# Two transformer blocks on one core: own buffers for each stage's first two weight units, their loads before the attention's end, and a later turn of the second row tile

## What is computed

```python
# block 0, per layer
proj = rmsnorm(x, g_pre_mix) @ w_in                      # 1024 x 3404
mix  = concat(top-k, forgetting, differential, window attention)
x = x + rmsnorm(mix @ w_out, g_post_mix)
x = x + rmsnorm(square(relu(rmsnorm(x, g_pre_mlp) @ w_up)) @ w_down, g_post_mlp)
x = x + sigmoid(x @ w_ple_gate) * (p_i @ w_ple_proj)
# block 1, per layer
z = x @ w_in_2 + b_in_2                                  # 1024 x 11648
mix = (sigmoid(ga) * (attn @ w_ap) + sigmoid(gb) * (silu(g) * retention @ w_rp)) @ w_out_2
x = layer_norm(ALPHA * x + mix)
x = layer_norm(ALPHA * x + (silu(x @ w_gate) * (x @ w_up)) @ w_down)
```

## Time and profile before

| | us |
|---|---|
| median of 3 runs | 2001.11 |
| profiled execution | 1996.49 |
| its span | 1994.7 |
| TensorE busy | 1905.3 (96%) |
| VectorE busy | 1172.4 (59%) |
| ScalarE busy | 887.9 (45%) |

### The profile page before, as it was taken

One profiled execution on the slowest core, in us unless ns is written; L12 is line 12 of the kernel. 1 busy time (PEld: TensorE's weight loads), 2 busy tenths in 40 slices (PEclk: granted clock), 3 DMA queues, 4 the chain that ended last, 5 costly groups with the idle time before them and its releaser, 6 DMA issues.

```text
span 1994.7 us, 25098 instructions
## 1 busy us (share of the span) xinstructions
PE 1905.3 (96%) x9135; PEld 1564.7 (78%) x9135; DVE 1172.4 (59%) x1372; ACT 887.9 (45%) x1071; POOL 82.3 (4%) x97
## 2 busy tenths in 40 slices
PE   7988999999899999999999989998999999989997
PEld 6777888778678887888877778886888877778885
DVE  5775555667765456556566565445556566574445
ACT  5544444555344445444345334443344355434442
POOL 5300000022100000000000000000000000000000
PEclk9989999999799999999999999999999999999998
DMA  7404555553755555664455644555663455645553
GB/s 260 141 15 154 189 183 166 177 190 113 86 190 195 182 174 181 216 213 124 143 189 173 224 152 160 186 184 190 213 215 122 147 185 191 209 149 164 186 186 106
DMA packets 194402, 340.25 MB, mean 171 GB/s; under 512 B 9338, under 2 KB 59418, under 8 KB 194316
## 3 DMA queue, kind: packets, MB, share of 16 engines
q1 hardware_dynamic: 189072, 327.76, 50.0%
q0 software_dynamic: 5120, 11.15, 3.1%
q10 hardware_dynamic: 123, 0.14, 0.0%
HBM read 333.24 MB, written 5.77 MB: 170 GB/s over the span
## 4 chain that ended last, share of the span: by engine, by line
PE 83%; DVE 8%; ACT 3%; DVEq 3%; issue 2%; DMA 1%; SPq 0%; ACTq 0%
PE G L580 18%; PE G L581 18%; PE G L585 18%; PE T L634 5%; PE A L580 4%; PE A L581 4%; PE A L585 4%; PE G L602 2%; PE G L596 2%; PE G L597 2%; DVE wlo L1544 2%; ACT whi L1090 2%; PE T L684 1%; PE A L694 1%; ACT arena L1090 1%
## 5 line engine op out<-in xcount | busy, mean ns | idle before, releaser
L1544 DVE TENSOR_TENSOR wlo<-raw,whi 128x2048 fp32r<-128x2048 f32 (+2 forms) x316 | 666.7, 2111 | 617.9 <-ACT whi L1090 617.4
L1090 ACT ACTIVATE whi<-raw 128x2048 fp32r<-128x2048 f32 (+3 forms) x320 | 566.0, 1769 | 647.1 <-PE G L585 523.8
L580 PE MATMUL G<-whi,XH 128*128 128x512 f32 (+1 forms) x1408 | 560.8, 398 | 8.3 <-DVE XL L1568 6.6
L581 PE MATMUL G<-whi,XL 128*128 128x512 f32 (+1 forms) x1408 | 550.3, 391 | 0.0
L585 PE MATMUL G<-wlo,XH 128*128 128x512 f32 (+1 forms) x1408 | 346.2, 388 | 0.0
L580 PEld LDWEIGHTS G<-whi,XH 128*128 128x128 f32 x1408 | 266.7, 189 | 64.8 <-issue 8.4
L581 PEld LDWEIGHTS G<-whi,XL 128*128 128x128 f32 x1408 | 266.7, 189 | 54.1 <-issue 1.9
L585 PEld LDWEIGHTS G<-wlo,XH 128*128 128x128 f32 x1408 | 263.9, 188 | 53.6
L634 PE MATMUL T<-ident,arena 128*128 128x128 f32 x812 | 120.7, 289 | 25.5 <-ACT arena L1090 18.1
L634 PEld LDWEIGHTS T<-ident,arena 128*128 128x128 f32 x812 | 99.3, 148 | 45.3 <-ACT arena L1090 15.3
L1090 ACT ACTIVATE arena<-T 128x512 f32<-128x512 f32 (+2 forms) x92 | 46.2, 550 | 151.2 <-PE T L634 150.9
(11 more groups left out here) (225 smaller groups left out, 2066.7 us busy)
## 6 DMA issues: line engine op xcount, KB each, us to landing
raw<-in_w_in SPq DMA_DIRECT2D x112, 1024.0 KB, 6.7
raw<-in_w_mlp_up SPq DMA_DIRECT2D x32, 1024.0 KB, 5.4
raw<-in_w_mlp_down SPq DMA_DIRECT2D x32, 1024.0 KB, 5.0
raw<-in_w_ffn_gate SPq DMA_DIRECT2D x44, 512.0 KB, 4.0
raw<-in_w_ffn_up SPq DMA_DIRECT2D x44, 512.0 KB, 5.0
raw<-in_w_ffn_down SPq DMA_DIRECT2D x44, 512.0 KB, 3.3
raw<-in_w_out SPq DMA_DIRECT2D x16, 1024.0 KB, 5.0
raw<-in_w_ret_proj SPq DMA_DIRECT2D x16, 1024.0 KB, 5.1
```

The lines of the kernel that those rows point to most:

```text
L580: nc.tensor.matmul(dst(m), hx[:, k0 + k, rows], hi[:, k, :], start=first and k == 0, stop=False)
L581: nc.tensor.matmul(dst(m), lx[:, k0 + k, rows], hi[:, k, :], start=False, stop=False)
L1090: return nc.scalar.activation(out_, in_, func, **kw)
L1544: tt(wlo[:, c % PARTS, 0:n], raw[:, slot, 0:n], whi[:, c % PARTS, 0:n].bitcast(F32), ALU.subtract).then_inc(s_lo.sem, 1)
```

## The change

1. Units 0, 1, 18, 19, 52 and 53 of a layer of block 0, and 0, 1, 60 and 61 of a layer of block 1, get a pair of buffers of their own (`FIRST`), laid over parts of the arena; the other units keep the two slots of `whi` and `wlo`. Counting semaphores are split accordingly (`s_hi1`, `s_lo1`). Some arena tiles move, and PB gets a tensor of its own.
2. `hi` and `lo` of these units move ahead of the norm in the queues of ACT and DVE; the halved `lo` goes.
3. Units 18 and 19 are loaded before SP's wait for the attention's end, so ahead of gains and p rows.
4. `first_chunk` turns tile 1 inside the half unit (0,1), between its high and its low products.
5. The layer loops of PE and SP, and SP's inner loops, are written out. PE's inner loops stay.
6. Three small constants (`relb`, `onehot`, `ok`) are loaded by POOL's queue and no longer by ACT's.

```diff
+FIRSTS = (0, U_MLP, U_PLE1 + 1), (0, V_FFN)
...
+        s_hi, s_lo = (Tally(sem(n), tuple(u - 2 * len(f) for u, f in zip((UNITS1, UNITS2), FIRSTS))) for n in ("s_hi", "s_lo"))
+        s_hi1, s_lo1 = (Tally(sem(n), tuple(2 * len(f) for f in FIRSTS)) for n in ("s_hi1", "s_lo1"))
...
+        def weights(blk, c, n):
+            at = first_no(blk, c)
+            hi, lo = (whi[:, c % PARTS], wlo[:, c % PARTS]) if at is None else FIRST[at % 2]
+            return hi[:, 0:n], lo[:, 0:n]
...
-            with sp.Fori(0, DEPTH) as L:
+            for L in range(DEPTH):
...
+                for k in range(2):
+                    unit(0, L, U_MLP + k, rows(up, L, 512 * k, UK, 0, COLS), UK, COLS, (U_MLP + k) % RAW)
+
                 sp.wait_ge(s_mix.sem, s_mix.at(0, L, 1))
...
                     for k in range(2):
-                        if (m, k) == (0, 1):
-                            row_turn(blk, L, t, 1, s_x, x)
                         pe.wait_ge(s_tfree.sem, s_tfree.at(blk, L, t + 2 * m + k + 1))
-                        half_unit(blk, L, m, c + k, XH, XL, UK * k, UK, bank_pair(group), k == 0, k == 1)
+                        half_unit(blk, L, m, c + k, XH, XL, UK * k, UK, bank_pair(group), k == 0, k == 1,
+                                  between=(lambda: row_turn(blk, L, t, 1, s_x, x)) if (m, k) == (0, 1) else None)
...
-            with pe.Fori(0, DEPTH) as L:
+            for L in range(DEPTH):
...
-                act.wait_ge(s_used.sem, s_used.at(blk, L, 4 * i + c - 1))
+                if (blk, L) != (0, 0) or c >= 2 * PARTS:
+                    act.wait_ge(s_used.sem, s_used.at(blk, L, 4 * i + before(blk, L, c) + 1))
...
-                hi(0, L, 0, U_OUT + 3)
+                his(0, L, 0, U_OUT + 3, U_MLP + 1)
...
-                hi(1, L, 0, V_OUT + 3)
+                his(1, L, 0, V_FFN, V_FFN + 1, V_OUT + 3)
...
-                lo(0, L, 0, U_OUT + 3)
+                los(0, L, 0, U_MLP, U_OUT + 3, U_MLP + 1)
...
-                lo_half(0, L, U_MLP, 0)
-                row_lo(0, L, T_N2, 0, 0, pre[:, 1, L])
-                lo_half(0, L, U_MLP, 1)
-                row_lo(0, L, T_N2, 0, 1, pre[:, 1, L])
+                row_los(0, L, T_N2, 0, pre[:, 1, L])
...
-                lo(1, L, 0, V_OUT + 3)
+                los(1, L, 0, V_FFN, V_FFN + 1, V_OUT + 3)
...
-                lo(1, L, 0, V_FFN)
-                row_lo(1, L, T2_FX, 0, 1)
                 dve.wait_ge(s_used.sem, s_used.at(1, L, V_OUT + 4))
                 residual(1, 1, 0).then_inc(s_evac.sem, 1)
+                row_lo(1, L, T2_FX, 0, 1)
                 row_spread(2, 1)
                 row_norm(6, 2, 1)
-                lo(1, L, 0, V_FFN + 1)
                 row_los(1, L, T2_FX, 1)
```

More of the change, by code:

```diff
@@ L115, in split_no, with first_no, ring_no, before @@
     return t - (T2_YA - T2_QK)
+FIRSTS = (0, U_MLP, U_PLE1 + 1), (0, V_FFN)
+def first_no(blk, c):
+    return next((2 * n + c - u for n, u in enumerate(FIRSTS[blk]) if c in (u, u + 1)), None)
+def ring_no(blk, c):
+    return c - sum(2 for u in FIRSTS[blk] if u < c)
+def before(blk, L, c):
+    n = first_no(blk, c)
+    if n is None:
+        return c - 2 if first_no(blk, c - 2) is None else c - 4
+    if n > 1:
+        return FIRSTS[blk][n // 2 - 1] + n % 2
+    last = (FIRSTS[0][-1] - UNITS1) if not blk or not L else (FIRSTS[1][-1] - UNITS2)
+    return last + n
 class Tally:
@@ L195, in program, with within @@
         gains = sb("gains", [P, 2, DM])
-        arena = sb("arena", [P, 17100])
+        with ExitStack() as shared:
+            def within(name, size, dt=F32R):
+                return shared.enter_context(nc.sbuf_tensor(name, [P, size], dt))
+            within("skip0", 2048, F32)
+            lo_b = within("lo_first1", UNIT)
+            within("skip1", 2048, F32)
+            hi_b = within("hi_first1", UNIT)
+            within("skip2", 4096, F32)
+            lo_a = within("lo_first0", UNIT)
+            within("skip3", 664, F32)
+            hi_a = within("hi_first0", UNIT)
+        FIRST = ((hi_a, lo_a), (hi_b, lo_b))
+        arena = sb("arena", [P, 17048])
         def room(lo, *dims):
@@ L388, in _ @@
             first(X[:, 1], xrows[:, 1], s_xin1)
-            with sp.Fori(0, DEPTH) as L:
+            for L in range(DEPTH):
                 w = a["w_in"]
-                with sp.Fori(0, 3) as i:
+                for i in range(3):
                     for c in range(2):
@@ L409, in _ @@
                     s_p.sem, 16)
[L410 to L413, removed]
+                for i in range(7):
                     for k in range(2):
@@ L455, in _ @@
                 w_in_chunks(0, V_RET, 7, RQ0, 1)
-                with sp.Fori(0, 3) as i:
+                for i in range(3):
                     w_in_chunks(i, V_RET + 2, 8, RQ0 + COLS)
                 w_in_chunks(0, V_RET + 14, 14, RQ0 + 7 * COLS, 1)
-                with sp.Fori(0, 4) as i:
+                for i in range(4):
                     w_in_chunks(i, V_GATE, 15, RQ0 + 8 * COLS)
@@ L487, in _ @@
                     gate_up(0, V_FFN + k, k, (V_FFN + k) % RAW)
-                with sp.Fori(0, FJ - 1) as i:
+                for i in range(FJ - 1):
                     for k in range(2):
@@ L1193, in _ @@
                 for m in range(TILES):
-                    ins = act_(room(12288, TILES, DM)[:, m], X[:, m, :], ACT.Square, accum_out=stat[:, 0, 0, m:m + 1])
+                    ins = act_(room(10240, TILES, DM)[:, m], X[:, m, :], ACT.Square, accum_out=stat[:, 0, 0, m:m + 1])
                 ins.then_inc(s_ss.sem, 1)
@@ L1278, in _ @@
                 for m in range(TILES):
[L1279 removed]
+                    ins = act_(room(10240, TILES, DM)[:, m], X[:, m, :], ACT.Square, accum_out=stat[:, 0, 3, m:m + 1])
                 ins.then_inc(s_ss.sem, 1)
@@ L1332, in _ @@
                 sigmoid(0, 1)
+                nxt, gain = ((0, L + 1), pre[:, 0, L + 1]) if L + 1 < DEPTH else ((1, 0), None)
+                his(*nxt, 0, 0, 1)
                 act.wait_ge(s_sgf.sem, s_sgf.at(0, L, 1))
@@ L1443, in _ @@
                 const(posi[:], a["positions"].rearrange("b (m p) -> p (b m)", p=P), s_const)
+                for dst, src in ((relb, "rel_bias_2"), (onehot, "c_onehot"), (ok, "c_ok")):
+                    const(dst, a[src], s_bconst)
                 pool.wait_ge(s_raw[0].sem, s_raw[0].at(0, 0, 1))
@@ L1692, in run_jobs @@
                         beside(q)
-            for t in (s_lo, s_tfree, s_evac, s_rlf, s_o, s_sgf):
+            for t in (s_tfree, s_evac, s_rlf, s_o, s_sgf):
                 dve.sem_inc(t.sem, t.credit)
```

106 lines of the change are left out of this document (48 added, 58 removed).

## The result

The changed kernel takes 1977.74 us in the median of 4 runs (1976.11 to 1978.85); the kernel before, on the same chip, took 1998.64 (1994.34 to 2001.44). The ratio is 0.9898, with a 95% interval of 0.9882 to 0.9913: 1.0% faster. The profiled execution took 1976.1, with a span of 1974.3: 20.4 less than before. Forecast were 1979 and a sum of 20.4. That the sum is exact is partly luck, as the table further down shows.

The account below looks back on a forecast made before the run. TensorE bounds the kernel, busy 1905 of 1995 us, so only its idle 89 us and lower-clock work can be won. Terms summed to 20.4 off the profiled 1996.5: 1976.1, or 1980.7 from the median; forecast 1979, range 1969 to 1990.

Parts of the forecast that it names:

- The sum: All openings' gains and losses together: 20.4 us off the profiled 1996.5.
- MLP, 1.9 and 3.0: MLP openings of layers 0 and 1: gains of 1.9 and 3.0 us, the second with the load issued during the attention.
- Gates, 3.0 each: Gate openings of both layers: XL no longer stands behind `lo(53)`; gain 3.0 us each, 6.0 together.
- FFN, 4.4 and 4.0: FFN openings of layers 0 and 1: x of tile 1 no longer behind `lo(60)`; gains 4.4 and 4.0 us.
- The new wait: Ahead of the FFN openings: `lo(60)` and `lo(61)` stand before `lo(59)`, so PE waits 1.4 us for it.
- Start of block 1, 0.6: Block 1, layer 0: (0,0) no longer waits for XL behind a half `lo`; gain 0.6 us.
- the "just hidden" step: Gated add of tile 0, after 4.5 us of next-layer `lo`: ends at 399.9, just hidden by its turn (399.7, 400.15).
- In-projections, -1.25 and -1.0: Kernel start and block 0's layer 1: x is there in time, so the later turn loses 1.25 and 1.0 us.
- Layer 1 of block 1, 2.7: Its opening: (0,0) no longer waits for `hi(0)`, nor 0.8 us put down to the jump; gain 2.7 us.
- the clock that I had counted only in a rival: Rival "more than forecast": full clock at every opening (1.4 at layer 1 of block 1), no new wait; 1973 or less, chance 0.12.
- The other jump: PE's second loop jump: no gain counted, as XL ended last there, 0.14 before the product.
- The slower rival: PE's written-out program: unhidden fetches cost 0.8 us each, 48 over 60 transfers, giving 2024; chance 0.04.

Follow-up runs that it names:

- Experiment 1: The changed kernel with tile 1's turn back between tile 0's two half units at all ten openings; 1983.81 us, ratio 0.9933 to the kernel before.
- experiment 6: The changed kernel with both the early turn at all ten openings and TensorE's layer loops as loops again; 1994.84 us, ratio 0.9981 to the kernel before.
- experiments 1 and 9: Experiment 1, and 9: the changed kernel with the early turn at block 0's two in-projections only; 1974.39 us, ratio 0.9886 to the kernel before.
- experiment 4: The kernel before with TensorE's two layer loops written out; 1998.42 us beside 1997.36, ratio 1.000.
- experiment 5: The changed kernel with TensorE's layer loops, and layer 1's loads of units 4 and 5 (block 0) held until unit 0 is used; one profile, 1989.31 us.
- experiment 3: The changed kernel with TensorE's two layer loops as loops again; 1989.67 us, ratio 0.9962 to the kernel before.
- experiment 7: The changed kernel with the loads of the MLP's first two units behind the wait for the attention's end again; 1995.43 us, ratio 0.9991 to the kernel before.

## Why the prediction was right

- **The sum held, and the method in the main.** Following three queues gave nine of ten openings within 0.7 us, though in two places below for another reason than mine. The waits forecast in place of the old ones are there: 1.33 for `lo` (forecast 1.4), 1.03 for XL with a gain (about 1), the wait for X at 9.3 (about 10). PE's busy time is 1897.8 (not under 1895), and there is no flood of "issue".
- **MLP, 1.9 and 3.0: measured 1.31 and 2.48.** The second is soft, as the old opening took 20.66 to 27.46 with the load's landing. In layer 0, less the 2.02 us by which the opening itself began later, the turn came at 189.72 (forecast 189.6) and (1,0) at 192.71 (192.4), and the old start of (1,0) was 194.05, not 194.2 (and 194.2 less 192.4 is 1.8, not 1.9). Experiment 1 adds that the late turn has no part in it: it costs 0.13 here.
- **Gates, 3.0 each: 2.81 and 2.85.** I put this down to `lo(53)` leaving XL's way. By experiments 1 and 6 only 1.0 to 1.2 comes from the queue (30.17 to 29.18 or 29.02) and 1.7 from the late turn, and the late turn alone is worth -3.2 there. The sum was right, and neither part has it alone.
- **FFN, 4.4 and 4.0: 4.05 and 3.76.** The new wait, the kept clock and the order are as written. The queue alone gives 0.7 and 2.0.
- **Start of block 1, 0.6: measured -0.08.** XL does leave the `lo`, but x of tile 0 comes 0.26 late behind the gated add (the "just hidden" step), and the late turn costs 0.32 (experiment 1: 24.21 for 24.53).
- **In-projections, -1.25 and -1.0: measured -1.49 and -0.85.** The second is shown as the late turn's by experiments 1 and 9 (25.04 and 25.03 with the early one). At the start the early turn gave 28.20, 28.25, 28.95 and 30.49 and the late one 29.00 to 30.84, so neither its share nor that of the constants (0 to 0.2 forecast) is resolved.
- **Layer 1 of block 1, 2.7: measured 4.38. This step was argued wrongly.** I let (0,0) wait for `hi(0)` until 1392.71 and gave the jump the 0.8 left. But `hi(0)` was done at 1388.67 (experiment 4): the 2.0 us between XL and (0,0) were all the jump's. Since I took both away, the size of that part came out right by luck: (0,0) starts 2.62 us behind the turn where it took 4.50. The 1.7 us beyond the forecast lie half ahead of the turn and half between (0,0) and (1,0), and there PEclk is 0.91 (1379 to 1383) where it was 0.58 (1393.5 to 1397.5), the clock that I had counted only in a rival.
- **The other jump I called free,** as XL ended last by 0.14: true in the kernel before, and in the new order it would have cost 6.67. The change writes the loops out, so the sum was safe from my error; with loops kept I would have forecast 1977 for the profiled execution where it took 1987.7. The Trainium skill ("Runtime: NRT & Kernel Launch", section "Instruction fetch mechanics") says that a taken branch whose target isn't at hand must fetch it before the engine goes on; the 2.55 and 4.48 of "issue" and experiment 5 agree. That weight transfers delay that fetch rests on experiment 5 and the instruction packets.
- **The slower rival had the cost on the wrong side.** Written-out code costs nothing here (experiment 4, and stages of 162.7 to 168.0 in MLP and FFN unchanged to 0.05); the jumps cost.
- **What I left out, mostly the clock, came to +4.4 in the mixers and -3.1 in the attention and at the end,** 1.3 in sum. With it 19.2 became 20.4. Why the clock fell in one and not in the other at equal idle isn't settled.

## What to carry to other kernels

A wait hides more than its own releaser: before you take it away, list what else lies under it (here a jump's fetch at one opening and tile 1's turn at another). What is won at one wait is lost at the next if that one isn't covered too (1.9 us at the old kernel's jump, lost to x of tile 1); the reverse edit in the old kernel then shows nothing, though the part is worth more than half the gain in the new one. Check the releaser that a profile names against the order of the program: twice here it was not the one that held PE. Put a filler behind the point where data would be waited for, and only there: where x was there in time, the same move lost 1.3 us, and where the filler's own operands came late, 3. Anything moved earlier in a queue must have its load moved at least as far.

## What the runs showed of the hardware

- A jump of TensorE's queue stood 1.80 to 2.97 us with the DMA quiet (2.09 and 2.97 in experiment 5, 2.55 in experiment 3, 1.80 in experiment 6, 2.79 in the kernel before), and 4.48 and 4.39 with the 16 engines full.
- After idle of 2.7 to 2.8 us products ran at half clock in one profile and at full in another, at the same place of the two kernels (PEclk 0.60 and 1.00); one such fall costs an estimated 1.5 to 1.7 us by PEclk, and stages with one came out up to 2.3 longer. That is the noise floor of any comparison by one trace here.
- A load of the MLP's first weights took 15.5 to 20.5 us behind the attention's end, where loads as large took 5.0 to 6.1 at layer 1's in-projection. SP issues it behind three other loads (in experiment 7 these took 4.8, 15.2 and 18.5 us); what held them isn't shown.
